# Sample attention of a hybrid decoder step: sixteen page transposes per request become matmuls with a 64-column selection matrix

## The reference, cut to what matters

```python
def sparse_core(q, k_sel, v_sel, valid):
    s = jnp.einsum("bthd,btkhd->bthk", q, k_sel, preferred_element_type=jnp.float32) * (DH_ATT ** -0.5)
    s = jnp.where(valid[:, :, None, :], s, -jnp.inf)
    p = jax.nn.softmax(s, axis=-1).astype(v_sel.dtype)
    o = jnp.einsum("bthk,btkhd->bthd", p, v_sel)
    return o.reshape(o.shape[0], o.shape[1], H_ATT * DH_ATT)
```

## Time and profile before

| what | value |
|---|---|
| median of 3 runs | 3372.75 us (3360.99 to 3374.34) |
| the profiled execution, its own time | 3372.75 us |
| its span in the profile | 3371.2 us |
| TensorE matmul busy (PE) | 3177.8 us, 94% |
| TensorE weight load busy (PEld) | 2934.2 us, 87% |
| VectorE busy (DVE) | 1718.2 us, 51% |
| ScalarE busy (ACT) | 892.1 us, 26% |
| GpSimd busy (POOL) | 667.1 us, 20% |
| mean granted TensorE clock | 0.967 |

### The profile page before, as it was taken

How to read it: one execution, slowest core, us unless ns; L and a number is a source line. 1 busy time by engine, 2 the same in 40 slices (tenths; PEclk the granted TensorE clock), 3 DMA queues, 4 the chain that set the end, 5 groups by cost and what they waited for, 6 DMA issues and landing times. The chain is left out here.

```text
span 3371.2 us, 51668 instructions
## 1 busy us (share of the span) xinstructions
PE 3177.8 (94%) x19665; PEld 2934.2 (87%) x19690; DVE 1718.2 (51%) x3021; ACT 892.1 (26%) x1596; POOL 667.1 (20%) x415
## 2 busy tenths in 40 slices
PE   6999999999898999999779898998999999999999
PEld 6999999999898999899545555557999999999999
DVE  5333333334589999997224444444744333333333
ACT  4111111112333332343333333342232111111111
POOL 1111211113433311233320000001211112111111
PEclk8999999999999999999779899998999999999999
DMA  3111111111222223122553345433431111111111
GB/s 98 51 44 37 50 44 44 44 44 57 82 79 76 78 79 87 39 84 72 170 173 113 114 131 190 132 110 128 133 118 43 45 37 50 44 44 44 44 37 66
DMA packets 253375, 265.47 MB, mean 79 GB/s; under 512 B 14527, under 2 KB 193314, under 8 KB 253214
## 3 DMA queue, kind: packets, MB, share of 16 engines
q1 hardware_dynamic: 247854, 254.64, 24.3%
q0 software_dynamic: 4128, 4.20, 0.4%
q10 hardware_dynamic: 1232, 4.46, 0.4%
HBM read 226.20 MB, written 37.05 MB: 78 GB/s over the span
## 5 line engine op out<-in xcount | busy, mean ns | idle before, releaser
L331 PE MATMUL bank<-h_hi,w_hi 128*128 128x362 f32 (+1 forms) x3384 | 1124.3, 332 | 38.2 <-DVE h_lo L218 19.9
L331 PE MATMUL bank<-h_lo,w_hi 128*128 128x362 f32 (+1 forms) x3384 | 1118.1, 330 | 0.0
L331 PE MATMUL bank<-h_hi,w_lo 128*128 128x362 f32 (+1 forms) x3384 | 1116.5, 330 | 0.0
L331 PEld LDWEIGHTS bank<-h_hi,w_hi 128*128 128x128 f32 x3384 | 642.6, 190 | 45.4 <-issue 25.1
L331 PEld LDWEIGHTS bank<-h_lo,w_hi 128*128 128x128 f32 x3384 | 643.2, 190 | 2.8
L331 PEld LDWEIGHTS bank<-h_hi,w_lo 128*128 128x128 f32 x3384 | 643.0, 190 | 0.0
L388 POOL TENSOR_TENSOR w_lo<-raw,w_hi 128x1024 fp32r<-128x1024 f32 x132 | 316.3, 2404 | 1290.6 <-ACT w_hi L483 1290.6
L550 DVE SCALAR_TENSOR_TENSOR x<-bank,x 128x362 f32<-128x362 f32 (+1 forms) x528 | 280.4, 535 | 213.8 <-PE bank L331 213.8
L331 PE MATMUL bank<-a_hi_ffn,w_hi 128*128 128x362 f32 (+1 forms) x1056 | 347.7, 329 | 5.5 <-DVE x L550 3.8
L331 PE MATMUL bank<-a_lo_ffn,w_hi 128*128 128x362 f32 (+1 forms) x1056 | 346.5, 328 | 0.0
L331 PE MATMUL bank<-a_hi_ffn,w_lo 128*128 128x362 f32 (+1 forms) x1056 | 346.3, 328 | 0.0
(11 more groups left out here) (356 smaller groups left out, 4110.5 us busy)
## 6 DMA issues: line engine op xcount, KB each, us to landing
raw<-in_w_ffn_in SPq DMA_DIRECT2D x88, 512.0 KB, 3.8
k_ring<-in_cache_k SPq DMA_DIRECT2D x128, 256.0 KB, 3.8
v_ring<-in_cache_v SPq DMA_DIRECT2D x128, 256.0 KB, 4.0
raw<-in_w_in SPq DMA_DIRECT2D x53, 512.0 KB, 4.8
raw<-in_w_ffn_out SPq DMA_DIRECT2D x44, 512.0 KB, 3.6
kept_g<-stage SPq DMA_DIRECT2D x24, 544.0 KB, 3.1
gate<-kept_g SPq DMA_DIRECT2D x24, 544.0 KB, 3.7
x<-x_kept SPq DMA_DIRECT2D x8, 544.0 KB, 4.4
```

Source lines behind the costliest of these rows:

```text
L331: mm = pe.matmul(out, left, right, start=(start and i == 0 and j == 0), stop=(stop and i == n - 1 and j == 2))
```

## The change

In the eighth slot the stationary operand stays the page of `ps`; the moving operand is no longer the identity in a transpose but `own`, a 128 x 64 matrix of zeros and ones that selects the 64 used rows, in an ordinary matmul. The result of one page is 64 columns wide, so eight pages fill a bank: three turns where there were five, and the eviction copies whole, contiguous turns. `own` is made once, by two VectorE copies from `ident` at the start of the stage. Strip 3 takes columns 32 to 63 of its block like strip 2, so its heads lie in the second half of the strip (rows 112 to 127); the padding of `rep`, `pts` and `qbd` and the two memsets go, and the eviction of `ot` copies strips 0 to 2 and strip 3 separately (four copies for two). All other parts stay.

```diff
-        [("pt", 0), ("pt", 1), ("pt", 2), ("pt", 3), ("pt", 4)],
+        [("pt", 0), ("pt", 1), ("pt", 2)],
...
-    pts = place("pts", [P, (PAGES + 1) * NS + 16], F32, ((PAGES + 1) * NS + 16) * 4)
-    qbd = place("qbd", [P, DEC_B * 4 * NS + 16], F32, 8192 + 64)
+    own = place("own", [P, NS], F32, NS * 4)
+    pts = place("pts", [P, PAGES + 1, NS], F32, (PAGES + 1) * NS * 4)
+    qbd = place("qbd", [P, DEC_B, 4, NS], F32, 8192)
...
-            if g < 4:
-                copy(pts[:, 4 * g * NS:(4 * g + 4) * NS].rearrange("p (g j c) -> p g j c", g=4, j=4),
-                     b.rearrange("p (g j c) -> p g j c", g=4, j=4)[:, :, :, 0:16]).then_inc(evicted[me], 1)
+            if g < 2:
+                copy(pts[:, 8 * g:8 * g + 8, :], b.rearrange("p (g n) -> p g n", n=NS)).then_inc(evicted[me], 1)
             else:
-                eng.wait_ge(tail_clear, 1)
-                copy(pts[0:DEC_T, PAGES * NS:(PAGES + 1) * NS].rearrange("p (j c) -> p j c", j=4),
-                     b[0:DEC_T, 0:P].rearrange("p (j c) -> p j c", j=4)[:, :, 0:16]).then_inc(evicted[me], 1)
+                copy(pts[0:DEC_T, PAGES, :], b[0:DEC_T, 0:NS]).then_inc(evicted[me], 1)
...
-                src = b[r, 0:P].rearrange("p (j c) -> p j c", c=32)[:, :, 8 * e:8 * e + DEC_T]
-                ins = copy(qT[r, :, at:at + 8], src)
+                src = b[r, 0:96].rearrange("p (j c) -> p j c", c=32)[:, :, 8 * e:8 * e + DEC_T]
+                copy(qT[r, 0:3, at:at + 8], src)
+                ins = copy(qT[r, 3, at:at + 8], b[r, 112 + 8 * e:120 + 8 * e])
...
-                        a = b * NS + 16 * j
-                        pe.matmul(bank[5][32 * j:32 * j + 32, 0:w], rep[:, a:a + 32],
+                        a = min(16 * j, 32)
+                        pe.matmul(bank[5][32 * j:32 * j + 32, 0:w], rep[:, b, a:a + 32],
...
                 elif kind == "pt":
+                    pe.wait_ge(own_made, 1)
                     pe.wait_ge(s_scaled, s + 1)
                     g = entry[2]
-                    if g < 4:
-                        for q in range(4):
-                            k = 4 * g + q
-                            mm = pe.transpose(tb[:, q * P:(q + 1) * P], ps[:, k * P:(k + 1) * P], ident[:, :])
+                    if g < 2:
+                        for q in range(8):
+                            k = 8 * g + q
+                            mm = pe.matmul(tb[:, q * NS:(q + 1) * NS], ps[:, k * P:(k + 1) * P], own[:, :],
+                                           start=True, stop=True)
                     else:
-                        mm = pe.transpose(tb[0:DEC_T, 0:P], ps[:, PAST:PAST + DEC_T], ident[:, :])
+                        mm = pe.matmul(tb[0:DEC_T, 0:NS], ps[:, PAST:PAST + DEC_T], own[:, :], start=True, stop=True)
...
-                    for g in range(5):
+                    for g in range(3):
                         wait_turn(pe, turn_of[("pt", s, g)])
-                    if s == 0:
-                        pe.wait_ge(tail_clear, 1)
...
-            dve.memset(pts[:, PAGES * NS:(PAGES + 1) * NS + 16], 0.0).then_inc(tail_clear, 1)
+            dve.tensor_copy(own[:, 0:48].rearrange("p (j c) -> p j c", c=16),
+                            ident[:, 0:96].rearrange("p (j c) -> p j c", c=32)[:, :, 0:16])
+            dve.tensor_copy(own[:, 48:NS], ident[:, 112:P]).then_inc(own_made, 1)
```

More of the change, by code:

```diff
@@ L598, in decoder_step @@
         bias_s = mem.at("bias_s", [NS, PAST + DEC_T], BF16, AT_B + 9216)
-        rep = mem.at("rep", [NS, DEC_B * NS + 16], BF16, AT_B + 9216 + 4128)
+        rep = mem.at("rep", [NS, DEC_B, NS], BF16, AT_B + 9216 + 4128)
         def dram(name, shape):
@@ L1890, in on_dve @@
             after(dve.tensor_scalar(dst, scores, BARRED * 1.25, BIG, ALU.is_gt, ALU.mult))
-        dve.memset(rep[:, DEC_B * NS:DEC_B * NS + 16], 0.0)
         for b in range(DEC_B):
-            dve.tensor_scalar(rep[:, b * NS:(b + 1) * NS].rearrange("p (h t) -> p h t", h=H),
+            dve.tensor_scalar(rep[:, b, :].rearrange("p (h t) -> p h t", h=H),
                               t8[0:NS, :].unsqueeze(1).to_broadcast([NS, H, DEC_T]), b8[:, 8 * b:8 * b + 1], None,
@@ L2394, in attention @@
     ps = place("ps", [P, PAST + DEC_T], F32, (PAST + DEC_T) * 4)
-    pts = place("pts", [P, (PAGES + 1) * NS + 16], F32, ((PAGES + 1) * NS + 16) * 4)
-    qbd = place("qbd", [P, DEC_B * 4 * NS + 16], F32, 8192 + 64)
-    qbd4 = qbd[:, 0:DEC_B * 4 * NS].rearrange("p (b j n) -> p b j n", b=DEC_B, j=4)
+    own = place("own", [P, NS], F32, NS * 4)
+    pts = place("pts", [P, PAGES + 1, NS], F32, (PAGES + 1) * NS * 4)
+    qbd = place("qbd", [P, DEC_B, 4, NS], F32, 8192)
     qmbd = place("qmbd", [P, DEC_B, 4, 32], F32, 4096)
@@ L2425, in attention @@
     used5, freed5 = sem("used5"), sem("freed5")
-    s_scaled, tail_clear = sem("s_scaled"), sem("tail_clear")
+    s_scaled, own_made = sem("s_scaled"), sem("own_made")
     s_max, s_exp, s_inv, s_norm = sem("s_max"), sem("s_exp"), sem("s_inv"), sem("s_norm")
@@ L2554, in _ @@
         def _(pool):
-            pool.memset(qbd[:, :], 0.0).then_inc(built0, 1)
+            pool.memset(qbd[:, :, :, :], 0.0).then_inc(built0, 1)
             pool.memset(qmbd[:, :, :, :], 0.0).then_inc(built0, 1)
@@ L2565, in _ @@
                         pool.wait_ge(built, h)
-                    pool.tensor_copy(qbd4[r, :, j, h * 8:h * 8 + 8],
+                    pool.tensor_copy(qbd[r, :, j, h * 8:h * 8 + 8],
                                      qT[r, j, SEQ:NT].rearrange("p (b t) -> p b t", b=DEC_B)).then_inc(built, 1)
@@ L2648, in _ @@
                     for j in range(4):
-                        a = b * NS + 16 * j
-                        pe.matmul(bank[5][32 * j:32 * j + 32, 0:w], rep[:, a:a + 32],
+                        a = min(16 * j, 32)
+                        pe.matmul(bank[5][32 * j:32 * j + 32, 0:w], rep[:, b, a:a + 32],
                                   bias_s[:, g * 512:g * 512 + w], start=True, stop=False, tile_position=(0, 32 * j))
                     for j in range(4):
-                        a = (4 * b + j) * NS + 16 * j
+                        a = min(16 * j, 32)
                         keys = kt4[:, g % 2, j, :] if g < 4 else kT[:, j, SEQ + 8 * b:SEQ + 8 * b + 8]
-                        mm = pe.matmul(bank[5][32 * j:32 * j + 32, 0:w], qbd[:, a:a + 32], keys, start=False,
+                        mm = pe.matmul(bank[5][32 * j:32 * j + 32, 0:w], qbd[:, b, j, a:a + 32], keys, start=False,
                                        stop=True, tile_position=(0, 32 * j))
@@ L2688, in _ @@
                         for j in range(4):
-                            a = k * NS + 16 * j
-                            left, right = (pts[:, a:a + 32], v_ring[:, k, j * P:(j + 1) * P]) if k < PAGES else \
-                                (pts[0:DEC_T, a:a + 32], vn[:, j * P:(j + 1) * P])
+                            a = min(16 * j, 32)
+                            left, right = (pts[:, k, a:a + 32], v_ring[:, k, j * P:(j + 1) * P]) if k < PAGES else \
+                                (pts[0:DEC_T, k, a:a + 32], vn[:, j * P:(j + 1) * P])
                             mm = pe.matmul(bank[5][32 * j:32 * j + 32, 0:P], left, right, start=(k == 0),
@@ L2739, in _ @@
                     if b >= 1:
-                        act.wait_ge(turned, turn_of[("pt", b - 1, 4)] + 1)
+                        act.wait_ge(turned, turn_of[("pt", b - 1, 2)] + 1)
                     act.copy(ps[:, g * 512:g * 512 + w], bank[5][:, 0:w]).then_inc(freed5, 1)
```

## The result

The changed kernel takes 3390.85 us (median of 8 runs, 3380.78 to 3410.64) against 3367.61 us for the kernel before (8 runs): ratio 1.0059, 95% interval 1.0039 to 1.0080, +20 us. The two medians of 8 lie 23 us apart, the ratio says 20; the record has further runs of the changed kernel, and over all 27 its median is 3386.42 us. A second measurement, 9 runs against 21 more of the kernel before, gave 1.0045 (1.0025 to 1.0064), +15 us.

What follows compares the result with a forecast made beforehand. TensorE was taken to set the attention stage's pace, waiting for short hand-offs. +10.7 us for doubled records less 0.3 ahead of `pv` gave +10.4 on 3372.75: 3383 us, own case 3380 to 3390, range in all 3368 to 3394.

Steps and rivals of the forecast that it cites:

- Two records for each fp32 matmul, one for each transpose: Eighth slot: 16 TensorE records a request become 32, 256 for the page matmuls against 128 for the transposes.
- 0.115 us a record, from the values of the prompt: Eighth slot: 32 records take 3.68 us, 3.78 with the last 8 columns, against 2.44; +10.7 us for eight requests.
- The last turn: End of the eighth slot: 8 columns of weights, two records, taken as 0.10 us.
- The hand-offs vanish, nothing new appears: Eighth slot: with three turns for five, no wait for evictions is left inside, and the eviction before `pv` stays hidden.
- the -0.3 us for two waits fewer: Ahead of `pv`: two waits fewer may give 0.04 us a request, -0.3 us in all; bounds 0 and -1.3.
- The small edits at nothing: `ot` copies (0.37 us more on ScalarE), `own` copies, `rep` memset and column offsets were to add no time.
- Rival 1: K page transfers on their own clock absorb up to 10.7 us of added time: 3373 to 3376 us; chance 0.10.
- Rival 2: Eighth slot: selection matmul needs one record a page, slot 1.8 us, -5 us in all: 3368 us; chance 0.05.
- Rival 3: Attention stage: denser matmuls raise the clock from a mean of 0.93, giving 3363 or 3343 us; chance 0.06.
- the forecast of +10.4 us: Whole kernel: +10.7 us from the eighth slots less 0.3 ahead of `pv`, 3383 us, +0.31%.
- rival 4: Low clock stretches fall elsewhere, each 7 us one losing up to 3.5 us; slower by over 0.5%; chance 0.14.
- All eight slots at a granted clock of 1.00: Eighth slots of the kernel before: all eight ran at the 2.4 GHz level, 2.44 us each on average.

Runs made afterwards that it cites:

- own_rounded: Changed kernel with the selection matmul's operands, probabilities and `own`, in fp32r: ratio 0.9999 (0.9987 to 1.0012) against the kernel before.
- layout_only: Changed kernel with the 128-column transposes and five turns of the kernel before: ratio 1.0012 (0.9997 to 1.0028) against the kernel before.
- after_16: Changed kernel with 16 more selection matmuls a request in the eighth slot: ratio 1.0129 (1.0107 to 1.0150), +43 us, against the kernel before.
- before_32: Kernel before with 32 more page transposes at the end of each eighth slot: ratio 1.0079 (1.0063 to 1.0094), +27 us.
- the filling: Identity transposes added where TensorE waits ahead of the slots of requests 0 and 2: changed kernel 1.0035, kernel before 1.0009 against the kernel before.
- rounded_filled: Changed kernel with fp32r selection matmul plus identity transposes in TensorE's waits ahead of slots 0 and 2: ratio 0.9988 (0.9976 to 0.9999) against the kernel before.

## Why the prediction was right, and where its size was off

- **Two records for each fp32 matmul, one for each transpose**: right, 256 and 128, shown again by own_rounded from the other side.
- **0.115 us a record, from the values of the prompt**: right, 0.116 us. The last turn took 0.21 us (1866.74 to 1866.95) for my 0.10, worth +0.9 us over eight requests.
- **The hand-offs vanish, nothing new appears**: right; no wait inside the slot. `pv` has its 0.17 us gap as before, so the -0.3 us for two waits fewer ahead of it did not come.
- **The small edits at nothing**: right within what layout_only can tell. The four output copies (L2506, L2507) last from 1796.16 to 1796.65, and `mot` loads its weights at 1797.15, unhindered: 0.12 us more than the two copies before, for the 0.37 I had allowed.
- **Rival 1, hidden behind the K pages**: wrong, as expected; one for one up to 40 us (after_16).
- **Rival 2, one record a page**: not this kernel, but exactly what own_rounded does.
- **Rival 3, the clock rises**: did not come; the stage's mean clock is 0.92 for 0.93. Slots of matmuls lay at 0.50 for their whole 7.38 us, and 13 more transposes cost what the change cost. The rule of the Trainium skill ("TensorE: Matmul & The Clock Gate", Part 4) that transposes do not count as activity would have favoured the change; no run here shows such an effect, and before_32 has a case against it (below).
- **Where the size was off**: the forecast of +10.4 us was 1.5 us short of the slots' +11.9, of which 0.9 is the last turn, 0.3 the gain ahead of `pv` that did not come, and the rest the 0.116 for 0.115 us a record. The other step is that I took the clock of the stage as unchanged and gave the price at the high level alone. The first trace has 90.7 us at the low level for 77.8, the second 86.5. That is rival 4 in size ("two such more decide", 7 us of time) and in kind (low stretches that lie elsewhere), at a chance of 0.14; that the forecast and this rival met inside the stated range is in part luck.
- **All eight slots at a granted clock of 1.00**: this was one draw and no property of the kernel. In six of the nine traces without the filling the slot of request 0 or of request 2, or both, lay wholly or partly low. A slot of transposes then takes 3.4 to 3.6 us, a slot of matmuls 7.38 us. By the table above this moved time between slots and rest and did not add to the stage's time in a way that the traces show.

What stays open: whether the change itself brings the 9 to 15 us more at the low level that its two traces have over the two of the kernel before, or whether that is scatter. The rest was 553.4 us in the first trace, 543.1 us in the second trace of the same code, and 539 to 547 us in nine further traces; it was 553.1 us once more, in rounded_filled, a kernel no slower than the one before. So such a long rest comes in a kernel that is no slower too, and scatter is the likelier reading; but the lower mean clock over 36 runs, though small, speaks for a part that belongs to the change. Two traces of the changed kernel are too few to decide it. Nor is it settled whether the first ratio, 1.0059, stands above the second by more than chance; their intervals overlap.

## What to carry to other kernels

Count records, not columns: an fp32 transpose of a 128x128 page and one of the two records of an fp32 matmul of 64 columns cost the same, so halving the output width by turning a transpose into a matmul loses unless the turns and evictions that it saves are worth more than the doubled records (here the slot was 1.5 us longer with two turns fewer). Do not take the clock that a stretch had in one trace as its own: in the next trace it may be at the other level. But do not price a change at the low level either because its lines lay low; add up the time at the low level over the whole stage, and compare the stages with half of it taken off. And before a small gain or loss is read off one trace, take a second trace of the same kernel: here the stage without its slots differed by 10 us between two of the same code.

## What the runs showed of the hardware that I had not expected

- The clock fell during a gap in which TensorE was busy for 1.40 of 4 us and was at 0.50 for the next 16 us, in the last 12 of which TensorE was busy throughout.
- The clock can rise in the middle of nothing but transposes. In before_32 the slot of request 0 begins at the low level, and the same transposes follow at the high one (TensorE; from 1775.5 us on it has transposes alone):

```profile
1775.31:1778.80 3.49, 3.49 (x18) 0.50 0.00 0
1779.00:1782.39 3.39, 3.39 (x34) 1.00 0.01 2
```

- The VectorE copy of 128x16, the second of the two that make `own`, took 1.68 us, beside GpSimd's clearing of `qbd` (1731.70 to 1733.50); the one of 128x48 ahead of it 0.20 us. In the timeline of VectorE after the change:

```profile
1731.74 0.20 DVE L2754 COPY own<-ident 128x48 f32<-128x48 f32 x1 [12.52 <-PEq L89]
1731.86 1.68 DVE L2756 COPY own<-ident 128x16 f32<-128x16 f32 x1
```

The first maximum ends about 0.5 us later by it (1.84 for 1.36 us after the stage's start), long before the first K page arrives. That the memset is the reason was not tried.
